# Taking the first two groups of each projection and feed-forward stage together, pair of k rows by pair of k rows

## The chip, the cores and the metric

The kernel runs on one core of one Trainium2 chip. The metric is the device time of one execution in microseconds, lower is better; several executions were timed, and one more was recorded by the hardware profiler.

## What is computed

The reference is one inference step of one decoder layer over 256 prompt tokens and 8 single sample tokens (264 columns together), with a model width of 2048. Cut to what matters here:

```
x = x + 0.5 * rms_norm(swiglu(rms_norm(x, g1pre), w_gu1, w_down1), g1post)
q, k, v of 16 heads = rms_norm(x, g_pre) @ w_in          # 2048 x 5120
mk, mv = split(rms_norm(mem, g_mem) @ w_mem_kv)          # 2048 x 1024
h = concat(norm(o_a), norm(o_b), norm(o_m))              # three kinds of attention
x = x + rms_norm(h @ w_out, g_post)                      # 2048 x 2048
x = x + 0.5 * rms_norm(swiglu(rms_norm(x, g2pre), w_gu2, w_down2), g2post)

def swiglu(x, w_gu, w_down):                             # w_gu 2048 x 11264, w_down 5632 x 2048
    g, u = split(x @ w_gu)
    return (silu(g) * u) @ w_down
```

All is float32.

## The kernel before

**Tiling.** Activations lie transposed, 16 tiles xT[:, k] of 128 features by 264 tokens. A matrix product is made in groups of 512 output columns. A *group* has eight *units*; a unit multiplies a pair of k tiles with 2 x 512 columns of weights into four PSUM banks (group 0 of a stage in four banks, group 1 in the other four, in turn). To keep float32 accuracy every operand is split in a high and a low part: xh and xl of the activations, wh and wl of the weights, and a unit does xh.wh + xl.wh + xh.wl. That is 4 blocks x 2 k tiles x 3 = 24 matmuls (L471 to L473).

**Weights.** The SP queue loads chunks of 1 MB (two units) into four `raw` slots; a chunk waits until the splits of the chunk four earlier are done (L312). `split` (ACT, L780) casts a unit of raw into one of four `wh` slots and waits until the unit that used the slot is done; `split` of DVE (L1111) makes wl = raw - wh. `AHEAD` is 3: units 0 to 2 of a stage are split in the stage before, and at unit c the split of unit c + 3 is issued. Part of the projection's splits are made by POOL (L1657).

**Activations.** xh comes from `upper` (ACT, L789), xl from `lower` (DVE, L1123, in the out stage L1120), pair by pair, and in group 0 TensorE waits for a pair's xl (`ready`). In the stages called mix (the projection w_in) and ffn2, x is also brought up to date on the way: DVE scales y by gain and 1/rms (`update_pair`, L1173) two pairs ahead, POOL adds it to xT (L1596). In out (w_out) DVE scales the heads (`normed`, L1525), with a reciprocal (L1520) ahead of the fifth and the seventh pair. The stages in order are mem (w_mem_kv, 256 columns), ffn1, mix, the attention, out, ffn2.

**The norm.** The matmuls take x without 1/rms; that factor is multiplied in when a bank is read. Squares of x are summed tile by tile on POOL (L1576, or ACT's squares L807 and POOL's sum L1589); after group 0 TensorE sums them over the partitions (`sum_partitions`, L488, in bank 7, or bank 0 in mem), ACT takes the root (L798), and TensorE waits for that before group 1, which takes the bank back. DVE inverts the root (L1129) and reads the banks (L1156 in mem, L1183 for gate in a feed-forward stage).

**Order.** Every engine's program is written out by hand; each engine runs its own in order. Group 0 of a stage start on ACT and on DVE is:

```
for c in range(8):                      # ACT
    upper(pair c)
    split(u0 + c + AHEAD)               # waits unit_used >= u0 + c
    squares_behind(name, c)             # squares of pair c - 1
for c in range(8):                      # DVE
    update_pair(c + 2)                  # mix and ffn2 only
    lower(pair c)
    split(u0 + c + AHEAD)
```

Group 1 then has splits only. In a feed-forward stage, groups 0 and 1 are gate and up of step 0; unit 16 is the first of the gate of step 1, and waits until DVE has read bank 0.

Of the kernel before, what the change touches and what calls it, by code (L numbers as in the profile page):

```python
# [91 lines left out]
def decoder_step(nc, x_prompt, x_sample, mem_prompt, win_k, win_v, sb_k, sb_v, mem_k, mem_v, page_table,  # L92
                 gains, w_gu, w_down, w_in, sb_bias, w_mem_kv, w_out, consts, outs):
    (y_prompt, y_sample, nwk_p, nwv_p, nsk_p, nsv_p, nmk_p, nmv_p, nwk_s, nwv_s, nsk_s, nsv_s) = outs
    with ExitStack() as ctx:
# [180 lines left out]

        def is_sb(h):
            return H_WIN <= h < H_WIN + H_SB
# [27 lines left out]
        def _(sp):  # L306
# [7 lines left out]

            for tile, src in ((gain_rows, gains), (ident, consts["ident"]), (ones, consts["ones"])):
# [3 lines left out]
            wmem = w_mem_kv[0].rearrange("(k p) n -> p k n", p=P)  # L319
            for n in range(4):  # L320
                load_chunk(n, n, wmem[:, 4 * n:4 * n + 4, 0:512], first=True)
# [11 lines left out]
            for n in range(4, 8):  # L333
                load_chunk(n, n % 4, wmem[:, 4 * (n - 4):4 * (n - 4) + 4, 512:1024])

            def ffn(l, base):
                wgu = w_gu[l][0].rearrange("(k p) n -> p k n", p=P)
                wdn = w_down[l][0].rearrange("(k p) n -> p k n", p=P)

                def gate_up(i, n):  # L340
                    for half in range(2):
                        for c in range(4):
                            load_chunk(n + 4 * half + c, c,
                                       wgu[:, 4 * c:4 * c + 4, bass.ds(i * 512 + half * D_FF, 512)])

                def down(i, n):
# [3 lines left out]
                gate_up(0, base)  # L350
# [11 lines left out]
            def load_in(n):  # L362

                g, c = divmod(n, 4)
                if n < 40:
# [94 lines left out]
        def _(pe):  # L460
# [24 lines left out]

            def sum_partitions(name, bank, a=0, width=TOK):
# [15 lines left out]
            group(0, N_MEM, 4, memp_done, None, xl_ready["mem"])  # L502
            pe.wait_ge(turn_read, KT)
            sum_partitions("mem", 0, width=N_MEM)
            pe.wait_ge(rooted, nth("mem"))
            group(8, N_MEM, 0, memp_done, None)
            pe.wait_ge(rows_loaded, 48)
# [16 lines left out]
            def ffn(l, base, name, guard_g, guard_u, bank_free):  # L524
# [55 lines left out]
            def in_group(g, par, guard=None):  # L580
                def before_last(j):
                    pe.wait_ge(in_read, (g - 2) * 4 + (j + 1))
                group(g * 8 + u_in, TOK, 4 * par, in_done, before_last if guard is None else guard,
                      xl_ready["mix"] if isinstance(g, int) and g == 0 else None)

            pe.wait_ge(rooted, nth("post1"))
            in_group(0, 0, lambda j: None)
            sum_partitions("mix", 7)
            in_group(1, 1, lambda j: wait_one(j, rooted, nth("mix")))
# [146 lines left out]
            for g in range(4):  # L736
                def guard(j):
                    if g == 0:
                        pe.wait_ge(o_read, HEADS)
                    elif g == 1:  # L740
                        wait_one(j, rooted, nth("out_m"))
                    else:
                        pe.wait_ge(out_read, 4 * (g - 2) + j + 1)
                group(u_out + 8 * g, TOK, 4 * ((g + 1) % 2), out_done, guard, xl_ready["out"] if g == 0 else None)
# [23 lines left out]
        def _(act):  # L768
            def split(c, i=0, per=24):

                if isinstance(i, int):
                    c, i = i * per + c, 0
                    if c >= unit_of(CH_END):
                        return
                raw_slot = (c // 2) % RAW_SLOTS
                if c % 2 == 0:
                    act.wait_ge(w_loaded[raw_slot], i * (per // 8 * 16) + 16 * (c // 8 + 1))
                if c >= UNIT_SLOTS or not isinstance(i, int):
                    act.wait_ge(unit_used, i * per + (c - UNIT_SLOTS + 1))
                act.activation(wh[:, c % UNIT_SLOTS], raw[:, raw_slot, 2 * (c % 2):2 * (c % 2) + 2], ACT.Copy  # L780
                               ).then_inc(hi_made, 1)
# [10 lines left out]
            def take_root(name, bank, size, before, half=False, width=TOK):  # L792

                act.wait_ge(summed, nth(name))
                if before is not None:
                    act.wait_ge(r_ready, nth(before))
                f = 4.0 if half else 1.0
                act.activation(root[:, 0:width], ps[bank][:, 0:width], ACT.Sqrt, scale=f / size,  # L798
                               bias=eps[:, 1:2] if half else eps[:, 0:1]).then_inc(rooted, 1)

# [18 lines left out]
            for c in range(8):  # L819
                for k in (2 * c, 2 * c + 1):  # L820
                    upper("mem", k, turn_read, k + 1, G_MEM)
                split(c + AHEAD)
            take_root("mem", 0, D_MODEL, None, width=N_MEM)
            for c in range(8, 16):
                split(c + AHEAD)
# [5 lines left out]
            def ffn(l, base, name, ready, ready_n, gain, before):  # L831
# [54 lines left out]
            for c in range(8):  # L886
                for k in (2 * c, 2 * c + 1):
                    upper("mix", k, x_ready["mix"], k + 1, G_PREM)
                split(u_in + c + AHEAD)
                squares_behind("mix", c)  # L890
            squares_behind("mix", 8)
            take_root("mix", 7, D_MODEL, "post1")
            for c in range(8, 32):
# [178 lines left out]
            for c in range(8):  # L1072
                for k in (2 * c, 2 * c + 1):
                    upper("out", k, x_ready["out"], k + 1, None)
                split(u_out + c + AHEAD)
            for g in range(1, 4):
                for c in range(8):
                    split(u_out + 8 * g + c + AHEAD)
                    if c % 2 == 1:
                        k = 4 * g - 4 + c // 2  # L1080
# [10 lines left out]
        def _(dve):  # L1091
# [11 lines left out]
            def split(c, i=0, per=24):  # L1103
# [6 lines left out]
                part = slice(2 * (c % 2), 2 * (c % 2) + 2)  # L1110
                dve.tensor_tensor(wl[:, c % UNIT_SLOTS], raw[:, (c // 2) % RAW_SLOTS, part],  # L1111
# [36 lines left out]
            for c in range(8):  # L1148
                for k in (2 * c, 2 * c + 1):
                    lower("mem", k, G_MEM)  # L1150
                split(c + AHEAD)
            invert("mem", r_post, N_MEM)
            dve.wait_ge(r_ready, nth("mem"))
            for j in range(4):
                block_ready(j, memp_done, 0, 7)
                dve.tensor_tensor(memkT[:, j], ps[4 + j][:, 0:N_MEM], r_post[:, 0:N_MEM], ALU.mult  # L1156
                                  ).then_inc(memp_read, 1)
            for c in range(8, 16):
                split(c + AHEAD)
# [17 lines left out]
            def ffn(l, base, name, gain, post_gain, then, bring_in=None):  # L1177
                u0 = unit_of(base)

                def take_gate(s, v):  # L1180
                    for j in range(4):
                        block_ready(j, g_done[l], s, v + 7)
# [27 lines left out]
                for c in range(8):  # L1210
# [4 lines left out]
                    split(u0 + c + AHEAD)  # L1215
# [5 lines left out]
                for c in range(8, 16):  # L1221
                    split(u0 + c + AHEAD)
# [29 lines left out]
            for c in range(8):  # L1252
# [3 lines left out]
                split(u_in + c + AHEAD)  # L1256
# [3 lines left out]
            def take_projection(g, a, dst, at):  # L1260

                for j in range(4):
                    block_ready(j, in_done, g + a, g * 8 + (u_in + 8 * a + 7))
# [4 lines left out]
            for c in range(8, 16):  # L1268
                split(u_in + c + AHEAD)
# [263 lines left out]
            for c in range(8):  # L1533
# [3 lines left out]
                split(u_out + c + AHEAD)  # L1537
            for g in range(4):
                if g > 0:
                    for c in range(8):  # L1540
                        split(u_out + 8 * g + c + AHEAD)
                for j in range(4):
                    block_ready(j, out_done, g, u_out + 8 * g + 7)
# [11 lines left out]
        def _(pool):  # L1555
# [35 lines left out]
            def update(name, before=None):  # L1591

                for k in range(KT + 4):
# [59 lines left out]
            def split(c, i=0):  # L1653

                pool.wait_ge(hi_made, i * 16 + (c + 1))
                part = slice(2 * (c % 2), 2 * (c % 2) + 2)
                pool.tensor_tensor(wl[:, c % UNIT_SLOTS], raw[:, (c // 2) % RAW_SLOTS, part],  # L1657
                                   wh[:, c % UNIT_SLOTS].bitcast(F32), ALU.subtract).then_inc(lo_made, 1)
# [133 lines left out]
```

## Time and profile before

| | |
|---|---|
| time, median of 3 runs | 2521.84 us (2518.68 to 2531.09) |
| the profiled execution | 2529.36 us, its span 2527.6 us |
| TensorE (PE) busy | 2201.4 us, 87% |
| VectorE (DVE) busy | 1542.8 us, 61% |
| ScalarE (ACT) busy | 1016.4 us, 40% |
| GpSimd (POOL) busy | 483.0 us, 19% |
| DMA | 468.31 MB, mean 185 GB/s |
| mean granted TensorE clock | 0.931 of full speed |

Busy time is an average over stages; the span goes from the first to the last instruction, and start times below count from its start. A DVE or POOL instruction's duration in the trace includes what it waited for access. Matmuls are pipelined, so that two follow each other faster than one lasts.

### The profile page before, as it was taken

What the parts mean: (1) busy time and instruction counts of PE and PEld (TensorE: products, weight loads), DVE (VectorE), ACT (ScalarE), POOL (GpSimd) and SP (SyncE); (2) the same over time, 40 slices, a digit from 0 to 9 for tenths busy, and PEclk for the clock granted to TensorE, in tenths of its full rate; (3) what the DMA queues carried; (4) which work ended last, traced back from release to release, by engine and by line L of the source; (5) the groups of instructions that cost most, each with busy time, mean ns of one, the idle gap of its engine ahead of it and who ended that gap; (6) DMA issues with size and microseconds to landing.
All of it is one profiled execution on the core that took longest, in us unless ns stands there. A gap on an engine that the chain in (4) does not pass through costs nothing.

```text
span 2527.6 us, 41312 instructions
## 1 busy us (share of the span) xinstructions
PE 2201.4 (87%) x16613; PEld 2080.1 (82%) x16613; DVE 1542.8 (61%) x3309; ACT 1016.4 (40%) x1300; POOL 483.0 (19%) x444
## 2 busy tenths in 40 slices
PE   6899999999999789655546766887999999999997
PEld 6799999999999779655532323787999999999996
DVE  6655555555555665578877856546555555555556
ACT  3344334344343443211116766334443443444443
POOL 4510000000000243535431211025000000000004
PEclk9999999999999989877767988898999999999998
DMA  7355555555555436577786964343555555555551
GB/s 251 134 184 184 171 185 180 182 184 184 179 172 184 150 121 231 169 245 257 239 287 222 290 211 159 139 161 113 177 178 184 184 175 185 179 180 183 184 182 54
DMA packets 230322, 468.31 MB, mean 185 GB/s; under 512 B 12689, under 2 KB 13714, under 8 KB 229346
## 3 DMA queue, kind: packets, MB, share of 16 engines
q1 hardware_dynamic: 227602, 460.78, 54.2%
q0 software_dynamic: 2528, 4.89, 0.5%
q8 instruction: 131, 2.15, 0.3%
q14 instruction: 61, 0.50, 0.1%
HBM read 456.40 MB, written 9.21 MB: 184 GB/s over the span
## 4 chain that ended last, share of the span: by engine, by line
PE 71%; DVE 13%; DMA 5%; POOL 4%; issue 3%; ACT 3%; SPq 1%; POOLq 0%; ACTq 0%; DVEq 0%
PE ps L471 23%; PE ps L472 23%; PE ps L473 22%; DVE k_cache L1305 6%; DMA k_cache<-win_k 2%; DVE vl L1469 2%; DMA k_cache<-sb_k 1%; POOL acc L1589 1%; ACT vh L1019 1%; DVE wl L1111 1%; PE ps L702 1%; DVE xl L1123 1%; ACT wh L780 1%; PE ps L704 1%; POOL wl L1657 1%
## 5 line engine op out<-in xcount | busy, mean ns | idle before, releaser
L471 PE MATMUL ps<-xh,wh 128*128 128x264 f32 (+1 forms) x3840 | 1122.1, 292 | 167.7 <-POOL wl L1657 109.2
L1111 DVE TENSOR_TENSOR wl<-raw,wh 128x1024 fp32r<-128x1024 f32 x605 | 749.1, 1242 | 758.6 <-ACT wh L780 758.4
L780 ACT ACTIVATE wh<-raw 128x1024 fp32r<-128x1024 f32 x656 | 690.5, 1058 | 1218.7 <-PE ps L473 989.8
L472 PE MATMUL ps<-xl,wh 128*128 128x264 f32 (+1 forms) x3840 | 1114.8, 290 | 0.0
L473 PE MATMUL ps<-xh,wl 128*128 128x264 f32 (+1 forms) x3840 | 1113.4, 290 | 0.0
L471 PEld LDWEIGHTS ps<-xh,wh 128*128 128x128 f32 x3840 | 748.6, 195 | 182.1 <-POOL wl L1657 113.8
L472 PEld LDWEIGHTS ps<-xl,wh 128*128 128x128 f32 x3840 | 747.8, 195 | 0.0
L473 PEld LDWEIGHTS ps<-xh,wl 128*128 128x128 f32 x3840 | 745.7, 194 | 0.0
L471 PE MATMUL ps<-hh,wh 128*128 128x264 f32 x1408 | 400.0, 284 | 0.0
L473 PE MATMUL ps<-hh,wl 128*128 128x264 f32 x1408 | 399.9, 284 | 0.0
L472 PE MATMUL ps<-hl,wh 128*128 128x264 f32 x1408 | 399.8, 284 | 0.0
L1642 POOL TENSOR_TENSOR gate<-gate,r_pre 128x264 f32<-128x264 f32 x88 | 85.3, 1001 | 1275.6 <-ACT gate L837 1275.6
L1305 DVE CUSTOM_DVE_ANT_0 k_cache<-k_cache,q_rows 128x128 f32<-128x128 f32 (+1 forms) x768 | 229.5, 366 | 76.5 <-DMA k_cache<-win_k 42.6
L471 PEld LDWEIGHTS ps<-hh,wh 128*128 128x128 f32 x1408 | 265.5, 189 | 0.0
L472 PEld LDWEIGHTS ps<-hl,wh 128*128 128x128 f32 x1408 | 265.2, 188 | 0.0
L473 PEld LDWEIGHTS ps<-hh,wl 128*128 128x128 f32 x1408 | 264.4, 188 | 0.0
L1657 POOL TENSOR_TENSOR wl<-raw,wh 128x1024 fp32r<-128x1024 f32 x51 | 128.8, 2543 | 224.5 <-ACT wh L780 224.4
L1469 DVE TENSOR_TENSOR vl<-v_cache,vh 128x1024 fp32r<-128x1024 f32 (+1 forms) x96 | 116.2, 1240 | 52.0 <-ACT vh L1019 51.6
L702 PE MATMUL ps<-vh,weights 128*8 128x512 f32 (+1 forms) x192 | 86.0, 448 | 58.4 <-DVE vl L1469 57.5
L1204 DVE TENSOR_TENSOR y<-y,ps 128x264 f32<-128x264 f32 x352 | 127.3, 422 | 5.1 <-PE ps L473 5.0
L702 PEld LDWEIGHTS ps<-vh,weights 128*8 128x8 f32 (+1 forms) x192 | 17.9, 93 | 113.7 <-DVE vl L1469 89.4
L1019 ACT ACTIVATE vh<-v_cache 128x1024 fp32r<-128x1024 f32 (+1 forms) x96 | 98.7, 1049 | 29.7 <-PE ps L704 20.0
(215 smaller groups left out, 1242.3 us busy)
## 6 DMA issues: line engine op xcount, KB each, us to landing
raw<-w_gu SPq DMA_DIRECT2D x176, 1024.0 KB, 4.9
raw<-w_down SPq DMA_DIRECT2D x88, 1024.0 KB, 5.0
raw<-w_in SPq DMA_DIRECT2D x40, 1024.0 KB, 6.4
k_cache<-sb_k SPq DMA_DIRECT2D x128, 256.0 KB
v_cache<-sb_v SPq DMA_DIRECT2D x128, 256.0 KB, 3.6
raw<-w_out SPq DMA_DIRECT2D x16, 1024.0 KB, 5.0
raw<-w_mem_kv SPq DMA_DIRECT2D x8, 1024.0 KB, 10.1
k_cache<-win_k SPq DMA_DIRECT2D x16, 384.0 KB
```

Source lines behind the costliest of these rows:

```text
L471: pe.matmul(out, w_hi, rh(k0 + kk), start=first and kk == 0, stop=False)
L472: pe.matmul(out, w_hi, rl(k0 + kk), start=False, stop=False)
L473: mm = pe.matmul(out, w_lo, rh(k0 + kk), start=False, stop=last and kk == 1)
L702: pe.matmul(out[0:8, :], weights[0:n, 2 * k + j, b], vh[slot][0:n, part], start=first, stop=False, skip_group_check=True)
L780: act.activation(wh[:, c % UNIT_SLOTS], raw[:, raw_slot, 2 * (c % 2):2 * (c % 2) + 2], ACT.Copy).then_inc(hi_made, 1)
L1019: act.activation(vh[slot][0:n], v_cache[0:n, tile % V_SLOTS], ACT.Copy).then_inc(vh_made, 1)
L1111: dve.tensor_tensor(wl[:, c % UNIT_SLOTS], raw[:, (c // 2) % RAW_SLOTS, part], wh[:, c % UNIT_SLOTS].bitcast(F32), ALU.subtract).then_inc( ...
L1204: dve.tensor_tensor(y[:, b], y[:, b], ps[4 * (q % 2) + j][:, 0:TOK], ALU.add).then_inc(y_added[l], 1)
L1305: return dve.tensor_tensor_reduce(keys, keys, q_rows[0:n, HD * q_head:HD * q_head + HD], 1.0, 0.0, ALU.mult, ALU.add, zb[0:n, col:col + 1])
L1469: dve.tensor_tensor(vl[slot][0:n], v_cache[0:n, tile % V_SLOTS], vh[slot][0:n].bitcast(F32), ALU.subtract).then_inc(vl_made, 1)
L1642: pool.tensor_tensor(gate[:, j], gate[:, j], r_pre[:], ALU.mult).then_inc(gate_ready[l], 1)
L1657: pool.tensor_tensor(wl[:, c % UNIT_SLOTS], raw[:, (c // 2) % RAW_SLOTS, part], wh[:, c % UNIT_SLOTS].bitcast(F32), ALU.subtract).then_inc ...
```

## The change

In each of the five stages the first two groups are no longer made one after the other but together: `two_groups` issues, for each pair c of k rows, unit 2c of group 0 (one half of the banks) and unit 2c + 1 of group 1 (the other half). A chunk of `raw` now holds both groups' columns of one pair of k rows (`load_pair`, `load_neighbours`, and `raw_unit`, which picks a unit's part). Beside each pair's casts, ACT and DVE issue two splits, of units 2c + 3 and 2c + 4. The sum over the partitions is issued ahead of the very last unit, into the free columns of banks whose group is done (`sum_beside`), and the root is read from there in two parts; TensorE doesn't wait for the root any more, but the reading of the banks does. POOL adds the squares two tiles sooner (`update`). In out, eight of ACT's squares of y stand in the third group.

```diff
+            def load_pair(n, c, weights, cols, first=False):
+                if not first:
+                    sp.wait_ge(lo_made, 2 * n - 6)
+                src = weights.rearrange("(k p) (g n) -> p g k n", p=P, n=512)[:, cols, 2 * c:2 * c + 2]
+                sp.dma_start(raw[:, n % RAW_SLOTS].rearrange("p (g k) n -> p g k n", g=2), src
+                             ).then_inc(w_loaded[n % RAW_SLOTS], 16)
...
+            def two_groups(v, width, banks, done, guard, ready, between):
+
+                for c in range(8):
+                    pe.wait_ge(ready, 2 * c + 2)
+                    for n in range(2):
+                        if c == 7 and n == 1:
+                            between()
+                        unit(v + 2 * c + n, (2 * c + n) % UNIT_SLOTS, lambda k: xh[:, k, 0:width],
+                             lambda k: xl[:, k, 0:width], 2 * c, banks[n], width, c == 0, c == 7, done[n], guard[n])
+
+            def sum_beside(name):
+
+                pe.wait_ge(squared[name], KT)
+                pe.matmul(ps[0][:, TOK:512], ones[:], acc[:, 0, 0:512 - TOK], start=True, stop=True,
+                          skip_group_check=True)
+                pe.matmul(ps[1][:, TOK:2 * TOK + TOK - 512], ones[:], acc[:, 0, 512 - TOK:TOK], start=True, stop=True,
+                          skip_group_check=True).then_inc(summed, 1)
...
-                group(u0, TOK, 0, g_done[l], guard_g, xl_ready[name])
                 bank_free()
-                sum_partitions(name, 7)
-                pe.wait_ge(rooted, nth(name))
-                group(u0 + 8, TOK, 4, u_done[l], guard_u)
+                two_groups(u0, TOK, (0, 4), (g_done[l], u_done[l]), (guard_g, guard_u), xl_ready[name],
+                           lambda: sum_beside(name))
...
# ACT, a feed-forward stage (mem, mix and out alike)
                 for c in range(8):
                     for k in (2 * c, 2 * c + 1):
                         upper(name, k, ready, ready_n + k + 1, gain)
-                    split(u0 + c + AHEAD)
                     if name != "ffn1":
                         squares_behind(name, c)
-                if name != "ffn1":
-                    squares_behind(name, 8)
-                take_root(name, 7, D_MODEL, before)
+                        if c == 7:
+                            squares_behind(name, 8)
+                    split(u0 + 2 * c + AHEAD)
+                    split(u0 + 2 * c + 1 + AHEAD)
+                root_beside(name, before)
                 silu(0)
-                for c in range(8, 16):
-                    split(u0 + c + AHEAD)
                 upper_h(0, 0)
...
# DVE, a feed-forward stage
                     for k in (2 * c, 2 * c + 1):
                         lower(name, k, gain)
-                    split(u0 + c + AHEAD)
+                    split(u0 + 2 * c + AHEAD)
+                    split(u0 + 2 * c + 1 + AHEAD)
                 invert(name, r_pre)
                 dve.wait_ge(r_ready, nth(name))
                 if l == 0:
                     dve.wait_ge(mem_stored, 16 * 4)
                 take_gate(0, u0)
-                for c in range(8, 16):
-                    split(u0 + c + AHEAD)
                 take_up(0, u0, 0)
...
# POOL
-                for k in range(KT + 4):
+                for k in range(KT + 2):
                     if k < KT:
                         pool.wait_ge(y_scaled[name], k + 1)
                         pool.tensor_tensor(xT[:, k], xT[:, k], y[:, k], ALU.add).then_inc(x_ready[name], 1)
-                    if before is not None and k % 2 == 1 and k >= 5:
-                        add_square(name, k - 5, before)
-                        add_square(name, k - 4, before)
+                    if before is not None and k % 2 == 1 and k >= 3:
+                        add_square(name, k - 3, before)
+                        add_square(name, k - 2, before)
```

## Rows read from the trace of the kernel before

**Rows 1.** Two stretches: busy us (xcount) of PE, PEld, DVE, ACT, POOL; clock, DMA, GB/s.

```profile
1722.00:1733.00 11.00, 8.17 (x52) 7.74 (x51) 9.82 (x11) 5.10 (x10) 8.34 (x10) 0.83 0.28 95
...
2000.00:2100.00 100.00, 100.00 (x825) 100.00 (x824) 52.88 (x66) 40.90 (x47) 7.76 (x8) 1.00 0.52 180
```

**Rows 2.** Timeline of PE: first matmul of unit 0, and of unit 16, by stage.

```profile
23.38 0.55 PE L471 MATMUL ps<-xh,wh 128*128 128x256 f32 x1 [6.83 <-DVE xl L1123]
...
89.00 0.39 PE L471 MATMUL ps<-xh,wh 128*128 128x264 f32 x1 [2.17 <-DVE xl L1123]
...
146.38 0.28 PE L471 MATMUL ps<-xh,wh 128*128 128x264 f32 x1
...
886.51 0.56 PE L471 MATMUL ps<-xh,wh 128*128 128x264 f32 x1 [8.73 <-issue]
...
951.11 0.28 PE L471 MATMUL ps<-xh,wh 128*128 128x264 f32 x1
...
1590.40 0.59 PE L471 MATMUL ps<-xh,wh 128*128 128x264 f32 x1 [3.98 <-DVE xl L1120]
...
1649.52 0.28 PE L471 MATMUL ps<-xh,wh 128*128 128x264 f32 x1
...
1710.21 0.59 PE L471 MATMUL ps<-xh,wh 128*128 128x264 f32 x1 [8.68 <-DVE xl L1123]
...
1774.92 0.28 PE L471 MATMUL ps<-xh,wh 128*128 128x264 f32 x1
```

**Rows 3.** Timelines of ACT and PE in ffn1: a split, units 2 and 4.

```profile
92.29 1.06 ACT L780 ACTIVATE wh<-raw 128x1024 fp32r<-128x1024 f32 x1 [2.12 <-PE ps L473]
...
96.79 0.39 PE L471 MATMUL ps<-xh,wh 128*128 128x264 f32 x1 [0.77 <-DVE xl L1123]
...
104.23 0.39 PE L471 MATMUL ps<-xh,wh 128*128 128x264 f32 x1 [0.88 <-DVE xl L1123]
```

**Rows 4.** Timelines of DVE, PE and ACT in ffn2, unit 2 to unit 4.

```profile
1711.21 0.88 DVE L1173 SCALAR_TENSOR_TENSOR y<-y,G,r_post 128x264 f32<-128x264 f32 x2
...
1721.53 0.39 PE L471 MATMUL ps<-xh,wh 128*128 128x264 f32 x1 [2.78 <-DVE xl L1123]
...
1726.34 1.06 ACT L780 ACTIVATE wh<-raw 128x1024 fp32r<-128x1024 f32 x1 [4.61 <-PE ps L473]
...
1727.43 1.23 DVE L1111 TENSOR_TENSOR wl<-raw,wh 128x1024 fp32r<-128x1024 f32 x1 [1.18 <-ACT wh L780]
1728.57 1.87 DVE L1173 SCALAR_TENSOR_TENSOR y<-y,G,r_post 128x264 f32<-128x264 f32 x2
1730.37 1.86 DVE L1123 SCALAR_TENSOR_TENSOR xl<-xT,G,xh 128x264 fp32r<-128x264 f32 x2
...
1732.29 0.39 PE L471 MATMUL ps<-xh,wh 128*128 128x264 f32 x1 [2.76 <-DVE xl L1123]
```

**Rows 5.** Timelines of ACT and PE in out, a turn without scaling.

```profile
1617.17 1.06 ACT L780 ACTIVATE wh<-raw 128x1024 fp32r<-128x1024 f32 x1 [5.96 <-PE ps L473]
...
1620.23 0.39 PE L471 MATMUL ps<-xh,wh 128*128 128x264 f32 x1 [0.25 <-DVE xl L1120]
```

**Rows 6.** Timeline of PE: unit 6 of mem, unit 2 of mix.

```profile
46.81 0.39 PE L471 MATMUL ps<-xh,wh 128*128 128x256 f32 x1 [0.42 <-DVE xl L1123]
...
896.30 0.45 PE L471 MATMUL ps<-xh,wh 128*128 128x264 f32 x1 [2.31 <-DVE xl L1123]
```

**Rows 7.** Timelines of ACT, DVE and PE around the root, in mem and ffn2.

```profile
51.08 1.28 ACT L798 ACT_TABLE_LOAD   x1
...
53.71 1.75 DVE L1129 RECIPROCAL r_post<-root 128x256 f32<-128x256 f32 x1 [1.39 <-ACT root L798]
55.49 1.42 DVE L1156 TENSOR_TENSOR memkT<-ps,r_post 128x256 f32<-128x256 f32 x4
...
77.54 7.86 DVE L1167 COPY xT<-ps 128x264 f32<-128x264 f32 x16
...
1750.18 0.71 PE L488 MATMUL ps<-acc,ones 128*128 128x264 f32 x2 [2.25 <-POOL acc L1589]
```

More of the change, by code:

```diff
@@ L275, in unit_of, with raw_unit @@
             return 2 * chunk
+        def raw_unit(c):
+            chunk, n = divmod(c, 2)
+            beside = CH_IN <= chunk < CH_IN + 8 or CH_OUT <= chunk < CH_OUT + 8
+            return raw[:, chunk % RAW_SLOTS, n:4:2] if beside else raw[:, chunk % RAW_SLOTS, 2 * n:2 * n + 2]
         def is_sb(h):
@@ L501, in _, with sum_memory @@
             pe.wait_ge(gains_ready, 1)
-            group(0, N_MEM, 4, memp_done, None, xl_ready["mem"])
             pe.wait_ge(turn_read, KT)
-            sum_partitions("mem", 0, width=N_MEM)
+            def sum_memory():
+                pe.wait_ge(squared["mem"], KT)
+                pe.matmul(ps[4][:, N_MEM:2 * N_MEM], ones[:], acc[:, 0, 0:N_MEM], start=True, stop=True,
+                          skip_group_check=True).then_inc(summed, 1)
+            two_groups(0, N_MEM, (4, 0), (memp_done, memp_done), (None, None), xl_ready["mem"], sum_memory)
+            pe.wait_ge(rows_loaded, 48)
             pe.wait_ge(rooted, nth("mem"))
-            group(8, N_MEM, 0, memp_done, None)
-            pe.wait_ge(rows_loaded, 48)
             pe.wait_ge(memp_read, 4)
@@ L735, in _ @@
             u_out = unit_of(CH_OUT)
[L736 to L744, printed above, removed]
+            two_groups(u_out, TOK, (4, 0), (out_done, out_done),
+                       (lambda j: wait_one(j, o_read, HEADS), lambda j: wait_one(j, rooted, nth("out_m"))),
+                       xl_ready["out"], lambda: None)
+            for g in range(2, 4):
+                group(u_out + 8 * g, TOK, 4 * ((g + 1) % 2), out_done,
+                      lambda j: pe.wait_ge(out_read, 4 * (g - 2) + j + 1))
             pe.wait_ge(out_read, 16)
@@ L779, in split @@
                     act.wait_ge(unit_used, i * per + (c - UNIT_SLOTS + 1))
-                act.activation(wh[:, c % UNIT_SLOTS], raw[:, raw_slot, 2 * (c % 2):2 * (c % 2) + 2], ACT.Copy
+                act.activation(wh[:, c % UNIT_SLOTS], raw_unit(c), ACT.Copy
                                ).then_inc(hi_made, 1)
@@ L799, in take_root, with root_beside @@
                                bias=eps[:, 1:2] if half else eps[:, 0:1]).then_inc(rooted, 1)
+            def root_beside(name, before):
+                act.wait_ge(summed, nth(name))
+                if before is not None:
+                    act.wait_ge(r_ready, nth(before))
+                act.activation(root[:, 0:512 - TOK], ps[0][:, TOK:512], ACT.Sqrt, scale=1.0 / D_MODEL, bias=eps[:, 0:1])
+                act.activation(root[:, 512 - TOK:TOK], ps[1][:, TOK:2 * TOK + TOK - 512], ACT.Sqrt,
+                               scale=1.0 / D_MODEL, bias=eps[:, 0:1]).then_inc(rooted, 1)
             def square(name, k, src, ready=None, n=0):
@@ L821, in _ @@
                     upper("mem", k, turn_read, k + 1, G_MEM)
-                split(c + AHEAD)
-            take_root("mem", 0, D_MODEL, None, width=N_MEM)
-            for c in range(8, 16):
-                split(c + AHEAD)
+                split(2 * c + AHEAD)
+                split(2 * c + 1 + AHEAD)
+            act.wait_ge(summed, nth("mem"))
+            act.activation(root[:, 0:N_MEM], ps[4][:, N_MEM:2 * N_MEM], ACT.Sqrt, scale=1.0 / D_MODEL, bias=eps[:, 0:1]
+                           ).then_inc(rooted, 1)
             for i in range(4):
@@ L888, in _ @@
                     upper("mix", k, x_ready["mix"], k + 1, G_PREM)
-                split(u_in + c + AHEAD)
                 squares_behind("mix", c)
-            squares_behind("mix", 8)
-            take_root("mix", 7, D_MODEL, "post1")
-            for c in range(8, 32):
+                if c == 7:
+                    squares_behind("mix", 8)
+                split(u_in + 2 * c + AHEAD)
+                split(u_in + 2 * c + 1 + AHEAD)
+            root_beside("mix", "post1")
+            for c in range(16, 32):
                 split(u_in + c + AHEAD)
@@ L1074, in _ @@
                     upper("out", k, x_ready["out"], k + 1, None)
-                split(u_out + c + AHEAD)
-            for g in range(1, 4):
+                split(u_out + 2 * c + AHEAD)
+                split(u_out + 2 * c + 1 + AHEAD)
+            for g in range(2, 4):
                 for c in range(8):
                     split(u_out + 8 * g + c + AHEAD)
-                    if c % 2 == 1:
-                        k = 4 * g - 4 + c // 2
+                    for k in ([c] if g == 2 else [8 + c // 2] if c % 2 == 1 else []):
                         square("postm", k, y, out_read, k + 1)
@@ L1154, in _ @@
             for j in range(4):
-                block_ready(j, memp_done, 0, 7)
+                block_ready(j, memp_done, 0, 14)
                 dve.tensor_tensor(memkT[:, j], ps[4 + j][:, 0:N_MEM], r_post[:, 0:N_MEM], ALU.mult
                                   ).then_inc(memp_read, 1)
-            for c in range(8, 16):
-                split(c + AHEAD)
             for j in range(4):
@@ L1653, in split @@
             def split(c, i=0):
[L1655 to L1658, printed above, removed]
+                pool.wait_ge(hi_made, c + 16 * i + 1)
+                c += 16 * i
+                pool.tensor_tensor(wl[:, c % UNIT_SLOTS], raw_unit(c), wh[:, c % UNIT_SLOTS].bitcast(F32),
+                                   ALU.subtract).then_inc(lo_made, 1)
             def scale_kv(g, block):
```

50 lines of the change are left out of this document (29 added, 21 removed).

## The prediction

> **What bounds the kernel now.** I read the page first (TensorE busy in 87% of the span), then the waits of TensorE, then its timeline around each stage start, and last the ACT, DVE and POOL timelines in the same stretches. In steady state TensorE is the bound: 825 matmuls in 100 us with no idle time, at the full granted clock [rows 1]. One unit is 24 matmuls, so it lasts 24 x 100 / 825 = 2.91 us, and ACT and DVE have room. The five stage starts differ. From the first matmul of unit 0 to the first of unit 16 the trace shows 57.4 us for ffn1, 64.6 for mix, 59.1 for out and 64.7 for ffn2 [rows 2], where 16 units of matmuls are 46.6. For mem I measure to the copies of xT that open the next stage: 77.54 - 23.38 = 54.2 us [rows 2, 7]. All of this excess is what the change could at best win, and it is in these five places alone; the attention stretch between is not touched.
>
> **What makes a stage start slow** is a ring, not a lack of engine time. There are four wh/wl slots and the splits run three units ahead. In the ACT program the casts of xh for pair c+1 stand behind the split of unit c+3, and that split waits until unit c-1 is done. So unit c+1 can't start before: unit c-1 ends, ACT splits (wh), DVE splits (wl), DVE scales y for a later pair (mix and ffn2 only), DVE makes two xl tiles. In ffn1 one turn of it reads: unit 0 starts at 89.00 [rows 2], ACT splits at 92.29, unit 2 starts at 96.79 and unit 4 at 104.23 [rows 3]: turns of 7.8 and 7.4 us for two units of 2.9. In ffn2 unit 2 starts at 1721.53, ACT splits at 1726.34, DVE splits at 1727.43, scales at 1728.57, makes xl at 1730.37, and unit 4 starts at 1732.29 [rows 4]: 10.8 us. Two things make it longer there. DVE's scaling of a pair took 1.87 us beside POOL's additions and 0.88 just before, with POOL idle [rows 4]. And after a stall of 2.78 us the clock fell: 4.81 us from the start of unit 2 to ACT's split, against 3.29 in ffn1; the granted clock of 1722 to 1733 was 0.83, a mix of 1.2 and 2.4 GHz [rows 1, 3, 4].
>
> The Trainium skill (SBUF — State Buffer, its account of the shared port pair) says that a VectorE instruction with two SBUF inputs and a GpSimd instruction that reads SBUF exclude each other for a whole instruction. The trace agrees with 1.87 against 0.88. If the lock were missed in the new order, each turn with scaling would be about 1.9 us shorter and the sum below some 15 us smaller; I keep the measured row.
>
> **The change, part by part.**
> *The order.* TensorE now does units 2c and 2c+1 on pair c. That doubles its work per pair (5.8 us) against DVE's, which is two splits and two xl tiles and, in mix and ffn2, two scalings. By engine totals TensorE would be the bound. But ACT and DVE issue both splits, of units 2c+3 and 2c+4, ahead of the casts of pair c+1, with three units of lookahead as before. The split of unit 2c+4 waits until unit 2c is done. So pair c+1, and with it unit 2c+2, waits on the end of unit 2c through the same chain as before; only unit 2c+1 runs meanwhile. The turn is the same length and still covers two units, but there are now seven turns (unit 0 to unit 14), where group 0 had three and a half and group 1 then ran freely at 2.91 us. A stage thus changes by 3.5 turns - 7 units (20.4 us) - the old gap for the sum and root, and breaks even near a turn of 6.5 to 7 us. The turns of mix and ffn2 are 10.8.
>
> *Prices of a turn.* With the clock full: 3.3 to ACT's split, and then to TensorE 4.2 with POOL active (7.4 - 3.3), 5.95 with scaling (1732.29 - 1726.34), and 3.06 with POOL idle (1617.17 to 1620.23) [rows 3 to 5]. After a stall like that of 2.78 us, 4.8 takes the place of 3.3. With scaling the stall is 10.8 - 4.5 - 2.9 = 3.3 us, or 9.2 - 3.1 - 2.9 = 3.2 if the clock had held, so I take the fall in those turns, and none at the 1.5 us stalls of the others.
>
> *ffn1:* 15.2 for two turns (89.00 to 104.23), 2 x 7.4 while POOL still squares, 3 x 6.4 after it: unit 14 starts at 49.3. Then 3.1 for unit 14 after a stall, 0.7 for the sum [rows 7], 2.9 for unit 15: 56.0. *mix:* 10.2 (9.8 before [rows 2, 6], and pair 1 is now cast behind unit 0), four turns of 10.75 with scaling, 9.0 after the last stall, 7.4: 69.6 + 6.7 = 76.3. *ffn2:* 11.3 (1710.21 to 1721.53), 43.0, 9.0, 7.4, 6.7: 77.4. *out:* POOL is idle; the scaling of a head pair is taken at the idle 0.8, so a chain is 3.9, and 5.7 in the two turns with a reciprocal of 1.8 [rows 4, 5, 7]: 9.5 + 9.0 + 8.7 + 9.0 + 8.7 + 6.3 + 6.3 = 57.5, + 6.0 = 63.5. *mem:* three turns as before, 46.81 - 23.38 = 23.4 [rows 2, 6], four of 6.4: unit 14 starts at 48.9.
>
> *The sum and root.* Before, TensorE waited for them between the groups. Now the sum stands ahead of unit 15, and POOL's squares (32 POOL operations of some 1 us) are done by then, so that wait goes; it is in the old lengths above. What is late next is the eviction: from the end of unit 14, ACT's split 1.06, root in two parts 0.8, reciprocal 1.75 [rows 7], the first tile 0.36 and hand-overs: 4.3 us, where the sum and unit 15 cover 3.6. So 0.7 us of stall before unit 16 in ffn1, mix and ffn2. Behind it, gate, silu, POOL's product and hidden run with no splits between; three prepared units (8.7 us) cover that, by about 1 us. In mem a table load of 1.28 us stands in it too [rows 7]: 1.06 + 1.28 + 0.5 + 1.75 + eight tiles 2.84 + 0.3 = 7.7 us from the end of unit 14 (48.9 + 3.3) to the copies of xT, so 59.9.
>
> *Taken at nothing:* the new weight layouts (the same bytes in chunks of 1 MB, issued four chunks ahead, with DMA share 0.28 [rows 1]; uncovered, one landing is 5 us by the page), the strided reads of raw, POOL's shorter lag (its additions are ready a turn ahead), and the eight squares in the third group of out, hidden under TensorE.
>
> **The sum:** mem 59.9 - 54.2 = +5.7; ffn1 56.0 + 0.7 - 57.4 = -0.7; mix 77.0 - 64.6 = +12.4; out 63.5 - 59.1 = +4.4; ffn2 78.1 - 64.7 = +13.4. Together +35 us. The profiled execution took 2529.4 us (span 2527.6), 7.5 above the median of the runs, so I add the 35 to the median: 2557 us.
>
> **Rivals.** (a) *The clock holds* in the long stalls (chance 0.16). Each of the 12 turns priced with 4.8 is 1.5 us shorter: +35 - 18 = +17, 2539 us. Against it: the stall is longer than the one of 2.78 after which it fell. (b) *The clock falls in the 1.5 us stalls too* (0.12), in 13 turns of mem and ffn1: +20 more, 2577 us. Against it: ffn1's stalls of up to 0.9 us left it full, and nothing between 0.9 and 2.3 was read. (c) *TensorE becomes the bound* (0.11), as its 5.8 us a pair against DVE's work suggests: it needs the casts and xl of pair c+1 to be ready when unit 2c+1 ends, which is a chain of under 2.9 us from the end of unit 2c. Then a stage is 16 units, a cold first one and the tail: mem -1, ffn1 -9, mix -15, out -10, ffn2 -14, together -49, 2473 us. The shortest chain in the trace is 3.06 [rows 5], with neither POOL nor scaling, so this decides only if I misread what the split waits for. (d) *Half of each* (0.08): POOL's lock misses DVE and the stalls stay under 2.3 us: about +5, 2527 us.
>
> **The numbers.** My forecast (the ring, clock falling with scaling) has 0.53. Within 0.5% (12.6 us, about what this kernel's runs can tell) lies (d). Forecast, (a) and (b) are slower by over 0.5%, all but a little of (a). Faster 0.11, same 0.10, slower 0.79. The range of 2534 to 2577 takes in (a) and (b) and leaves out (c), (d) and little else.
>
> **What will show it.** TensorE's timeline should have its stalls ahead of the even units 2 to 14 of each stage start, ended by DVE's xl tiles, of about 1.5 us in ffn1 and 3 in mix and ffn2, and none ahead of odd ones; ACT's split of unit 2c+4 should start as unit 2c ends. TensorE's wait for POOL's acc ahead of the sum should be gone in four stages. The granted clock of mix's and ffn2's starts should be near 0.8. I am wrong if unit 2c+2 follows 2c+1 without a gap, or if the fall of the clock isn't there.

## The result, and the profile after

| | before | after |
|---|---|---|
| time, median | 2522.25 us (4 runs) | 2564.15 us (4 runs, 2563.04 to 2568.49) |
| ratio, 95% interval | | 1.017 [1.0152, 1.0188] |
| span of the profiled execution | 2527.6 us | 2563.5 us |

The change costs 42 us; 35 were forecast. The page of the changed kernel (busy us, share of the span, instructions) shows as much work as before on DVE and ACT, and TensorE busy for a smaller share of a longer span:

```profile
PE 2215.1 (86%) x16619; PEld 2090.6 (82%) x16619; DVE 1541.4 (60%) x3309; ACT 1016.6 (40%) x1303; POOL 469.6 (18%) x444
```

TensorE ran six matmuls more but was busy for 13.7 us more: its matmuls last longer where the granted clock is low. Over the five stage starts it was busy for 16.8 us more and idle for 26.9 us more, so most of the time is in waits, and the rest in the low clock that goes with them. The timeline of TensorE at the start of mix, these being the first matmuls of units 0, 2, 4 and 6, then of 12, 14 and 16, all of which waited (they answer to [rows 2, 6]):

```profile
897.53 0.56 PE L498 MATMUL ps<-xh,wh 128*128 128x264 f32 x1 [7.76 <-issue]
...
908.35 0.39 PE L498 MATMUL ps<-xh,wh 128*128 128x264 f32 x1 [2.01 <-DVE xl L1175]
...
917.66 0.59 PE L498 MATMUL ps<-xh,wh 128*128 128x264 f32 x1 [3.20 <-DVE xl L1175]
...
928.32 0.59 PE L498 MATMUL ps<-xh,wh 128*128 128x264 f32 x1 [3.19 <-DVE xl L1175]
...
959.98 0.39 PE L498 MATMUL ps<-xh,wh 128*128 128x264 f32 x1 [1.42 <-DVE xl L1175]
...
967.51 0.39 PE L498 MATMUL ps<-xh,wh 128*128 128x264 f32 x1 [1.41 <-DVE xl L1175]
...
975.44 0.36 PE L498 MATMUL ps<-xh,wh 128*128 128x264 f32 x1 [1.16 <-DVE qT L1315]
```

The waits of TensorE over the same stretch, grouped (us in total, times, longest), with those of units 8 and 10, which are not shown above:

```profile
PE ps L498 <- DVE xl L1175: 17.4, 7, 3.2
PE ps L498 <- issue: 7.8, 1, 7.8
PE ps L498 <- DVE qT L1315: 1.2, 1, 1.2
```

What to see here: seven stalls, all ahead of even units, all ended by an xl tile; no odd unit waits, nothing in this stretch waits for POOL's sum any more, and one new short wait stands ahead of unit 16. The turn from unit 6 to unit 8 of ffn2 answers to [rows 4], here from the timelines of PE, ACT and DVE:

```profile
1764.32 0.59 PE L498 MATMUL ps<-xh,wh 128*128 128x264 f32 x1 [3.19 <-DVE xl L1175]
...
1768.89 1.06 ACT L822 ACTIVATE wh<-raw 128x1024 fp32r<-128x1024 f32 x1 [6.67 <-PE ps L500]
1769.86 0.91 ACT L831 ACTIVATE xh<-xT,G 128x264 fp32r<-128x264 f32 x2
...
1769.98 1.23 DVE L1163 TENSOR_TENSOR wl<-raw,wh 128x1024 fp32r<-128x1024 f32 x1 [4.59 <-ACT wh L822]
1771.13 1.96 DVE L1224 SCALAR_TENSOR_TENSOR y<-y,G,r_post 128x264 f32<-128x264 f32 x2
1773.01 1.85 DVE L1175 SCALAR_TENSOR_TENSOR xl<-xT,G,xh 128x264 fp32r<-128x264 f32 x2
...
1774.92 0.59 PE L498 MATMUL ps<-xh,wh 128*128 128x264 f32 x1 [3.21 <-DVE xl L1175]
```

It is the ring of the prediction, link by link: unit 6 ends, ACT's split of unit 10 starts (4.6 us after the unit's start), and only then come the casts of pair 4 and DVE's split, scaling and xl: 10.6 us for two units. Two stretches, mix and ffn2, by busy time of PE, PEld, DVE, ACT and POOL, then clock, DMA share and GB/s:

```profile
897.00:966.00 69.00, 52.49 (x336) 51.13 (x336) 37.71 (x39) 23.85 (x41) 20.85 (x25) 0.83 0.32 107
1734.00:1795.00 61.00, 45.87 (x287) 44.60 (x286) 32.02 (x34) 20.95 (x36) 18.31 (x22) 0.81 0.31 104
```

DVE, ACT and POOL are all far from full; each waits for another. By stage, from the timelines, first matmul of unit 0 to first of unit 16 (for mem to unit 0 of ffn1):

| stage | before | after | change | forecast |
|---|---|---|---|---|
| mem | 65.6 | 76.7 | +11.0 | +5.7 (to the copies of xT) |
| ffn1 | 57.4 | 59.0 | +1.6 | -0.7 |
| mix | 64.6 | 77.9 | +13.3 | +12.4 |
| out | 59.1 | 63.7 | +4.6 | +4.4 |
| ffn2 | 64.7 | 77.9 | +13.1 | +13.4 |

That is +43.7 before rounding; all the rest of the span is 7.8 us shorter in this pair of executions (4.4 of it in the attention), which leaves the 35.9 between the spans. The attention, from unit 16 of mix to unit 0 of out, varies by itself: 626.1 to 641.0 us in the traces of the eight kernels with AHEAD = 3, and 636.3 and 640.2 in two executions of one kernel. So a difference of a few us between two totals says less than the same difference in a stage start.

### The profile page after: what moved, and what is told of

The parts are those of the page before. It is cut to its first block, busy times and chain, and to the rows that moved or that the text cites. A ratio compares the mean times of both kernels' runs of the same rounds, so it can differ in the third digit from the quotient of the medians.

```text
span 2563.5 us, 41323 instructions
## 1 busy us (share of the span) xinstructions
PE 2215.1 (86%) x16619; PEld 2090.6 (82%) x16619; DVE 1541.4 (60%) x3309; ACT 1016.6 (40%) x1303; POOL 469.6 (18%) x444
## 4 chain that ended last, share of the span: by engine, by line
PE 69%; DVE 16%; DMA 6%; ACT 4%; issue 3%; POOL 2%; SPq 1%; POOLq 0%; ACTq 0%; DVEq 0%
PE ps L498 22%; PE ps L499 22%; PE ps L500 22%; DVE k_cache L1354 6%; DMA k_cache<-win_k 3%; DVE wl L1163 2%; DVE xl L1175 2%; DVE vl L1518 2%; ACT wh L822 2%; DMA k_cache<-sb_k 1%; DMA v_cache<-win_v 1%; POOL acc L1639 1%; DVE y L1224 1%; ACT vh L1072 1%; PE ps L747 1%
## 5 line engine op out<-in xcount | busy, mean ns | idle before, releaser
L1518 DVE TENSOR_TENSOR vl<-v_cache,vh 128x1024 fp32r<-128x1024 f32 (+1 forms) x96 | 116.6, 1244 | 49.8 <-ACT vh L1072 49.3
L1072 ACT ACTIVATE vh<-v_cache 128x1024 fp32r<-128x1024 f32 (+1 forms) x96 | 98.5, 1049 | 27.8 <-PE ps L749 18.2
```

The lines of the kernel that those rows point to most:

```text
L1072: act.activation(vh[slot][0:n], v_cache[0:n, tile % V_SLOTS], ACT.Copy).then_inc(vh_made, 1)
L1518: dve.tensor_tensor(vl[slot][0:n], v_cache[0:n, tile % V_SLOTS], vh[slot][0:n].bitcast(F32), ALU.subtract).then_inc(vl_made, 1)
```

## Experiments

Each ran beside the kernel before on the same chip; ratios are to that, with the 95% interval in brackets. Line numbers differ a little between kernels.

**1. The casts a pair ahead, in the new order.**

```diff
# ACT (a feed-forward stage; mem, mix, out alike)
+                for k in (0, 1):
+                    upper(name, k, ready, ready_n + k + 1, gain)
                 for c in range(8):
-                    for k in (2 * c, 2 * c + 1):
+                    for k in ((2 * c + 2, 2 * c + 3) if c < 7 else ()):
                         upper(name, k, ready, ready_n + k + 1, gain)
                     ...
                     split(u0 + 2 * c + AHEAD)
                     split(u0 + 2 * c + 1 + AHEAD)
# DVE: lower(pair c + 1) and bring_in(c + 3) in place of lower(pair c) and bring_in(c + 2)
# POOL: the squares lag four tiles, as before the change
```

> The changed kernel with one thing moved: in all five stage starts ACT casts xh and DVE makes xl of pair c+1 ahead of the splits of units 2c+3 and 2c+4 (DVE's scaling one pair earlier too; POOL's additions lag four tiles again, since two would deadlock with it). My theory, the ring: pair c+1 no longer waits for the end of unit 2c, so the stalls ahead of the even units go and each stage start is near 16 units of 2.91 us plus a cold first unit: ffn1 about 50 us (59.0 in the changed kernel), out 50 (63.7), mix and ffn2 50 to 56 (77.9 each), mem a few us less. In all 70 us less than the changed kernel, about 2490, faster than the kernel before. Rival 1: DVE's work per pair (two splits, two scalings, two xl tiles, slowed by POOL) is the bound and the order hardly matters: the stages stay within 5 us, total about 2555. Rival 2: what is saved at the ring comes back at the first reading of the banks or in POOL: total about 2520.

Measured: 2484.89 us, 0.9861 [0.9835, 0.9887]. The start of mix in TensorE's timeline, unit 0 and the next first matmul that waited, unit 16:

```profile
884.55 0.56 PE L498 MATMUL ps<-xh,wh 128*128 128x264 f32 x1 [8.73 <-issue]
...
936.08 0.36 PE L498 MATMUL ps<-xh,wh 128*128 128x264 f32 x1 [0.96 <-DVE qT L1331]
```

No unit between waited: 51.5 us in place of 77.9. The other starts took 51.3 (ffn1), 48.4 (out) and 50.2 (ffn2). The same instructions in another order save 79 us against the changed kernel, so it was the order, not DVE's work: both rivals fall. (The longer lag of the squares, which had to come with it, is worth nothing by itself: experiment 8.) Mem took 69.7 us for 76.7.

**2. The casts a pair ahead, in the old order** (the same edit of ACT and DVE in the kernel before, whose POOL lag is four anyway).

> The kernel before (groups one after the other) with the casts of pair c+1 ahead of the split of unit c+3. Ring theory: group 0 is then bound by what DVE does per unit: in out 2.8 us, so it runs at TensorE's pace (-9 us), in ffn1 and mem about 3.1 to 3.4 (-3 each), in mix and ffn2 5 us a unit as before (0 to -3 each). Total about -15 to -20: 2503 us. It shows that the new grouping is worth its other 15 us only with the order mended. Rival: if the order alone were the whole matter, this kernel would come within 5 us of the other one with casts ahead.

Measured: 2521.29 us, 1.0009 [0.9993, 1.0025]: no change, where 15 to 20 us were expected. Out answered (49.6 us for 59.1), and mem (61.6 for 65.6), and the other stages took most of it back. In ffn1 group 0 was done sooner, and then TensorE waited for POOL's squares: 57.6 us for 57.4. In mix (68.8 for 64.6) and ffn2 (69.9 for 64.7) the casts now wait for POOL. The first line is TensorE's wait for the sum in ffn1, the others are ACT's and POOL's timelines in mix:

```profile
116.85 1.22 PE L488 MATMUL ps<-acc,ones 128*128 128x264 f32 x2 [6.36 <-POOL acc L1595]
...
899.80 0.51 ACT L789 ACTIVATE xh<-xT,G 128x264 fp32r<-128x264 f32 x1 [3.06 <-POOL xT L1615]
...
901.87 0.72 ACT L807 ACTIVATE sq<-xT 128x264 f32<-128x264 f32 x2
...
902.35 2.39 POOL L1608 TENSOR_TENSOR acc<-acc,sq 128x264 f32<-128x264 f32 x2 [1.89 <-ACT sq L807]
904.69 1.63 POOL L1615 TENSOR_TENSOR xT<-xT,y 128x264 f32<-128x264 f32 x2
905.66 0.51 ACT L789 ACTIVATE xh<-xT,G 128x264 fp32r<-128x264 f32 x1 [3.07 <-POOL xT L1615]
```

Earlier casts made a second ring of 5.86 us a pair (899.80 to 905.66): ACT's squares, POOL's additions of squares, POOL's additions to xT, ACT's casts, split and squares. One unit of 2.9 us a pair can't cover it; two units of 5.8 can, and experiment 1 shows that they do.

**3. AHEAD = 2 in the new order.** One constant; the second split of a pair is then of unit 2c + 3, which waits for the end of unit 2c - 1.

```diff
-AHEAD = 3
+AHEAD = 2
```

> The changed kernel with AHEAD = 2 in place of 3, all else as it is: the second split of a pair is then of unit 2c+3 and waits for the end of unit 2c-1, so both units of pair c run beside the chain. Ring theory: ffn1, out and mem lose their stalls and mix and ffn2 keep under 1 us each (chain of 6 us against 5.8): the stage starts are as short as with the casts ahead, though splits are made less far ahead, 60 to 70 us less than 2564. Rival: less lookahead can only make the starts slower, and the steady part of the feed-forward stages, with two prepared units instead of three over the reading of the banks, adds up to 2 us in each of 20 steps: above 2564. The stage starts and the steady part are read apart in the trace.

Measured: 2469.89 us in a single execution. The waits of TensorE from 870 to 920 us, the start of mix:

```profile
PE ps L498 <- issue: 7.8, 1, 7.8
PE ps L498 <- DVE xl L1175: 0.5, 2, 0.3
```

Two waits of 0.3 us are left of the seven, which is the expected 6 us of chain against 5.8 of cover. The stage starts took 49.2, 50.3, 49.8 and 50.8 us, and mem 61.6 for 76.7. Behind the starts TensorE was busy for 723.1 of 726 us (ffn1) and 723.9 of 725 (ffn2). From unit 16 to the last unit that has xh as its operand a feed-forward stage took 675.2 us for 674.1: the rival's loss in the steady part is 1.1 us a stage, and not 2 us in each step. Less lookahead is faster here, since what counts is not how many units are prepared but which unit's end the casts stand behind. Timed again:

> The changed kernel with AHEAD = 2 once more, timed: 2470 us, 0.980 of the kernel before, if the single look was representative.

Measured: 2474.94 us, 0.9801 [0.9776, 0.9827]. It has the lowest median of the versions that were timed several times; experiment 7 is as fast within the intervals.

**4. Extra matmuls in the long stalls.**

```diff
+            def fill(n):
+                for _ in range(n):
+                    pe.matmul(ps[7][:, 384:512], ones[:], ident[:], start=False, stop=False, skip_group_check=True)
...
                 for c in range(8):
+                    if c in filled:      # mix and ffn2: 1 to 5; out: 2 and 4
+                        fill(10)
                     pe.wait_ge(ready, 2 * c + 2)
```

> The changed kernel with ten extra small matmuls (ones x ident into unused columns of a bank) in the long stalls: ahead of units 2 to 10 in mix and ffn2 and ahead of units 4 and 8 in out. They add nothing that is needed. If the fall of the clock after a long stall lengthens the turn (4.8 us in place of 3.3 from a unit's start to ACT's split), the granted clock stays full and the turns of mix and ffn2 go from 10.7 to about 9.2 us: -15 us in all, 2549. Rival: the turn's length has nothing to do with the clock, or the extra matmuls don't hold it: 10.7 us a turn stays and the time is 2564 or above.

Measured: 2550.49 us, 1.0129 [1.0103, 1.0154], against 1.017 of the changed kernel. Units 4, 6 and 8 of mix in TensorE's timeline, ACT's split behind the start of unit 4, and a stretch over them as above:

```profile
918.66 0.39 PE L498 MATMUL ps<-xh,wh 128*128 128x264 f32 x1 [0.99 <-DVE xl L1181]
...
921.95 1.06 ACT L828 ACTIVATE wh<-raw 128x1024 fp32r<-128x1024 f32 x1 [5.41 <-PE ps L500]
...
927.98 0.39 PE L498 MATMUL ps<-xh,wh 128*128 128x264 f32 x1 [0.97 <-DVE xl L1181]
...
937.33 0.39 PE L498 MATMUL ps<-xh,wh 128*128 128x264 f32 x1 [0.99 <-DVE xl L1181]
...
917.00:947.00 30.00, 26.07 (x214) 25.31 (x213) 20.09 (x21) 10.69 (x18) 11.16 (x14) 1.00 0.31 105
```

The granted clock is 1.00 (2.4 GHz) in place of 0.83, and a turn takes 9.3 us in place of 10.7, near the 9.2 of the prediction's rival (a). From the start of an even unit to ACT's split it is 3.3 us in every turn of mix and ffn2 from unit 2 on, where the changed kernel has 4.6 to 4.8 in seven of them and 5.7 to 5.8 in two. Mix is 6.8 us shorter, ffn2 8.2, out 4.1. These 19.1 us are the evidence: of the totals, 13.7 us apart, the intervals just touch. The fall of the clock is part of the ring's price, and work that is of no use buys it back.

**5. POOL's additions of the squares cut to 8 columns** (mix and ffn2; their sums are not computed).

```diff
-                    pool.tensor_tensor(acc[:, 0], acc[:, 0], sq[:, k % 2], ALU.add).then_inc(squared[name], 1)
+                    n = 8 if name in ("mix", "ffn2") else TOK
+                    pool.tensor_tensor(acc[:, 0, 0:n], acc[:, 0, 0:n], sq[:, k % 2, 0:n], ALU.add
+                                       ).then_inc(squared[name], 1)
```

> The changed kernel with POOL's additions of the squares (of the norms ahead of mix and ffn2) cut to 8 of 264 columns, so that sum is not computed. It measures how much of a turn of 10.7 us is DVE waiting beside POOL: DVE's scaling of a pair should fall from 1.9 us towards 0.9, its xl tiles stay near 1.9 where POOL's additions to xT now fall on them, the chain from ACT's split to unit 2c+2 goes from 5.95 to about 5 us, and mix and ffn2 are each 5 to 8 us shorter: about 2552. If the stall then drops below the point at which the clock falls, 1.5 us a turn more. Rival: the share of POOL is small and the turns stay within 0.3 us.

Measured: 2553.81 us in a single execution, near the 2552 expected. DVE's and POOL's timelines in mix:

```profile
923.82 0.92 DVE L1224 SCALAR_TENSOR_TENSOR y<-y,G,r_post 128x264 f32<-128x264 f32 x2
924.66 1.86 DVE L1175 SCALAR_TENSOR_TENSOR xl<-xT,G,xh 128x264 fp32r<-128x264 f32 x2
...
924.36 1.87 POOL L1648 TENSOR_TENSOR xT<-xT,y 128x264 f32<-128x264 f32 x2
```

The scaling of a pair costs 0.92 us with POOL's long additions of squares away, and the xl tiles still 1.86 beside POOL's additions to xT: the doubling follows POOL's instructions. Mix is 9.1 us shorter and ffn2 9.6, a little over the 5 to 8 expected; the total moved by less (the spans by 11.4 us), as the attention took 6.1 us more in this execution. All six stalls of 2.17 or 2.18 us were still followed by a unit at the low clock (turns of 9.6 to 9.8 us where scaling goes on); two of 1.98 and 2.02 us, each in the turn after such a unit, were not (8.3).

**6. AHEAD = 2 in the old order.**

> The kernel before with AHEAD = 2 and nothing else. The run of the changed kernel with AHEAD = 2 was 2% faster than the kernel before: this one tells whether that is the constant alone or needs the two groups together. My theory: in the old order DVE's work per unit (5 us in mix and ffn2) and POOL's squares (31 us in ffn1) bind group 0 however the ring stands, as they did with the casts ahead: within 0.5% of the kernel before, 2510 to 2522. Rival: the constant is the gain, and this kernel comes near 2470 as well.

Measured: 2495.62 us, 0.9889 [0.9863, 0.9915]. Neither my theory (2510 to 2522) nor the rival (2470) is right: the constant alone gives 1.1%, and the grouping gives another 0.9% on top (0.9801). Stage starts: mem 61.8, ffn1 58.2, mix 57.7, out 49.3, ffn2 59.0. My reading, which no run isolates: unlike in experiment 2, the casts keep their place behind the squares, so POOL's part of the ring is as it was, while the split they stand behind waits for a unit one earlier. What is left in ffn1 is POOL again: TensorE waited 4.13 us for the sum. With two groups together the same constant leaves 47.7, 51.1, 48.6 and 51.6 us.

**7. Both mends.**

> Both mends in the changed kernel: casts a pair ahead, and AHEAD = 2. The ring is cut by either, so at the stage starts there is nothing more to win; what AHEAD = 2 saved beyond the casts ahead (2470 against 2485) should be the tails (one split fewer ahead of the root, and in mem no long stall that lets the clock fall): 2468 to 2475, the same as AHEAD = 2 alone. Rival: the two add up, 2455.

Measured: 2478.93 us, 0.9826 [0.9804, 0.9849]; stage starts 49.2, 50.3, 49.5, 49.3 us. The interval overlaps that of AHEAD = 2 alone, and the two mends don't add up.

**8. The squares' lag.** The changed kernel with KT + 4 and k >= 5 in POOL's `update`, as before the change.

> The changed kernel with POOL's additions of the squares lagging four tiles behind x again, as in the kernel before, and nothing else. I took the shorter lag at nothing: the squares are wanted only ahead of unit 15, some 60 us into a stage. 2564 within 0.3%, 1.017 of the kernel before. Rival: POOL's order matters to the ring through x_ready or through what falls beside DVE's instructions, and mix and ffn2 move by more than 2 us each.

Measured: 2568.01 us, 1.0211 [1.0186, 1.0236]. It overlaps the 1.017 [1.0152, 1.0188] of the changed kernel, if barely, so the shorter lag is worth nothing to a few us. In the traces the five stage starts add up to 354.7 us, against 355.1: nothing.

**9. The root ahead of the last split, in mem.**

```diff
# ACT
                 split(2 * c + AHEAD)
-                split(2 * c + 1 + AHEAD)
+                if c < 7:
+                    split(2 * c + 1 + AHEAD)
             act.wait_ge(summed, nth("mem"))
             ...
+            split(15 + AHEAD)
# DVE alike, its split(15 + AHEAD) behind the copies of xT
```

> The changed kernel with, in mem alone, the last split (of unit 18) moved behind the root on ACT and behind the copies of xT on DVE. The tail there ran split 1.06, table load 1.28, root, reciprocal, memkT, and TensorE waited 3.05 us ahead of its transposes, which then ran at the low clock (0.82 us per tile against 0.52 before). If the wait let the clock fall, a wait of about 2 us will leave it up or fall later: the transposes are 3 to 5 us shorter, plus the 1 us itself: 5 us less from mem to ffn1, 2559. Rival: the transposes are slow for another reason (their reads of the banks, DVE's copies), and only 1 us is saved: 2563.

Measured: 2561.64 us, 1.0176 [1.015, 1.0201], no difference from the changed kernel. The first line is TensorE's first transpose of x in the changed kernel and the stretch over them; the others are of this kernel, tiles 0, 3 and 4:

```profile
80.33 0.41 PE L563 MATMUL ps<-ident,x_rows 128*128 128x128 f32 x2 [3.05 <-DVE memkT L1209]
...
81.00:93.00 12.00, 12.00 (x46) 6.74 (x45) 6.81 (x17) 0.00 (x0) 0.00 (x0) 0.50 0.00 1
```

```profile
79.96 0.41 PE L563 MATMUL ps<-ident,x_rows 128*128 128x128 f32 x2 [1.05 <-DVE memkT L1212]
...
81.50 0.44 PE L563 MATMUL ps<-ident,x_rows 128*128 128x128 f32 x2
...
82.03 0.69 PE L563 MATMUL ps<-ident,x_rows 128*128 128x128 f32 x2
```

The wait fell from 3.05 to 1.05 us and mem to ffn1 is 74.6 us for 76.7: the 2 us of the wait, and not the 5 expected. The clock fell all the same, after the fourth tile. That it fell later is not the edit's doing: in experiments 4 and 8, where mem is as in the changed kernel and the wait 3.05 us, it fell after the fourth tile too. With AHEAD = 2 (the run timed again) the wait is 1.05 us as well, and there the clock held:

```profile
71.00:84.00 13.00, 10.34 (x65) 7.14 (x65) 9.14 (x23) 3.52 (x7) 4.00 (x2) 1.00 0.02 6
```

That the transposes take 0.82 us a tile at half the clock and 0.52 at the full one is shown; what makes it fall is not settled. The length of the wait alone doesn't decide. The transposes didn't bring the clock back either: in the changed kernel TensorE was busy with them for all 12 us of the stretch from 81 to 93 at half clock, where in mix each unit at the low clock, of 5.4 us at most, was followed by one with a granted clock of 0.93 or more.

## Why the prediction was right, point by point

**The ring** was right, and experiments 1 and 3 cut it in two ways that share the unit whose end the casts of pair c + 1 stand behind: 79 and 89 us less. The stalls are where the prediction put them, ahead of even units, 1.4 to 1.7 us without scaling while POOL works, 0.3 to 0.5 with POOL idle (mem and ffn1), and 3.0 to 3.2 with scaling.

**The prices of a turn** held, with their forecasts in brackets: 10.6 to 10.9 us with scaling in five turns of mix and ffn2 (10.75), 9.0 and 7.5 for the last two of mix (9.0, 7.4), 6.3 to 6.5 in mem and ffn1 with POOL idle (6.4). One turn each of mix and ffn2 took 11.8, as the low clock lasted for the whole unit of 5.4 us, and one of mix 9.3, as the clock held after a stall of 2.01 us. The clock's share, 4.8 for 3.3 us, was shown by experiment 4, and POOL's share by experiment 5. The Trainium skill (SBUF — State Buffer, on the shared port pair) says that a VectorE instruction with two SBUF inputs and a GpSimd instruction that reads SBUF exclude each other. The trace of experiment 5 agrees: a pair of DVE's instructions takes 0.92 us beside POOL's additions of 8 columns, and 1.86 beside additions of 264.

**That mix, out and ffn2 came within 1 us is in part luck.** In ffn2 the first turn took 9.3 us for the 11.3 forecast, and the four with scaling 44.0 for 43.0; in out two turns missed by 0.9 us in opposite directions; the stretch from unit 14 to unit 16 took 7.9 us for 7.4 in ffn1, mix and ffn2.

**The sum and root.** TensorE's wait for the sum is gone in all four stages that had it, and in ffn1, mix and ffn2 a wait of 1.11 to 1.16 us ahead of unit 16 stands in its place (0.7 forecast), as these lines of ffn2 show, ACT's last split, the two roots, DVE's reciprocal and gate:

```profile
1806.56 1.06 ACT L822 ACTIVATE wh<-raw 128x1024 fp32r<-128x1024 f32 x1 [2.23 <-PE ps L500]
1807.52 0.45 ACT L848 ACTIVATE root<-ps,eps 128x248 f32<-128x248 f32 x1
1807.87 0.27 ACT L849 ACTIVATE root<-ps,eps 128x16 f32<-128x16 f32 x1
...
1808.79 1.79 DVE L1181 RECIPROCAL r_pre<-root 128x264 f32<-128x264 f32 x1
1810.62 1.45 DVE L1234 TENSOR_TENSOR gate<-ps,r_pre 128x264 f32<-128x264 f32 x4
...
1811.16 0.36 PE L498 MATMUL ps<-xh,wh 128*128 128x264 f32 x1 [1.11 <-issue]
```

The steady part behind it lost nothing, as forecast (674.1 us for 674.0 from unit 16 to the last unit on xh).

**What was mis-sized** is mem, and with it ffn1. To the copies of xT mem cost +4.7 us (58.8 against 54.2; 5.7 forecast), but the sum stopped there. TensorE's transposes of x, behind the wait of 3.05 us, ran at half the clock, which is 6.4 us more from the first copy to unit 0 of ffn1 (17.8 against 11.5), and ffn1 then began at the low clock too: unit 0 to unit 2 took 9.8 us for 7.8, which is why ffn1 is +1.6 and not -0.7. Together about 8 us, more than the whole error of 7. The five starts gave +43.7 for the +35.2 forecast; that the spans differ by just 35.9 is luck, from the 7.8 us that this execution was shorter elsewhere. Why the clock fell in mem stays open (experiment 9).

**My picture of the ring was too simple** in one respect that the prediction didn't need: with the casts moved ahead in the old order I expected DVE to be the bound, and it was POOL, in a second ring (experiment 2). AHEAD = 2 in the old order then gave more than my account of it (27.8 us for at most 13) and less than the rival's, and I give the reason above from the order of the programs, without a run that isolates it.

## What to carry to other kernels

When work per step is doubled to hide preparation, look at which instruction the preparation of the next step stands behind in its engine's program: here each extra split pushed the next casts behind the end of a unit of the current step, so the turn kept its length and there were twice as many. Add up one whole turn across all engines, not the busy time of each. The remedy is order (prepare the next step ahead of the refill of slots, or, with four slots, look ahead by two units and not by three), and only with it did the new grouping pay: 0.980 of the kernel before, against 1.017 without and 0.989 for the old grouping with the same constant.

## What the runs showed of the hardware

In mix and ffn2 of the changed kernel, stalls of 3.0 to 3.2 us with two units of matmuls between them (7.4 to 8.8 us) left the granted clock at 0.83 and 0.81 on average over the stretches shown; ten matmuls of 128 columns in each stall, of no other use, brought it to 1.00. Over the traces of all twelve executions, no stall of 1.0 to 1.67 us ahead of a unit of a stage start was followed by the low clock and every one of 2.67 us or more was; of those between, some were (1.72, 1.81 and six of 2.17 or 2.18 us) and some weren't (2.01, 2.28, 2.65 us). A wait of 1.05 us ahead of a run of small transposes was followed by the low clock in one kernel and by the full one in three executions of two others.

Two instructions of DVE with two inputs each in SBUF took 1.9 to 2.0 us beside POOL's additions and 0.9 without them or with POOL's cut to 8 columns, so a chain that runs through DVE is priced with what POOL does at that time.
